# Splitting the input projection's operands engine by engine, and latent queries laid out head by head with their vector step reordered

## The reference, cut to what matters

```
u    = rms_norm(h, ln) @ w_in          # 2048 -> [q latent 512 | kv latent 512 | rotary key 64 | gate 2048]
q    = rms_norm(c_q, ln_q)  @ w_q_up   # 16 heads x (128 plain + 64 rotary)
kv   = rms_norm(c_kv, ln_kv) @ w_kv_up # 16 heads x (128 key + 128 value)
k    = concat([k_plain, k_pe for every head])
q, k = rms_norm(q, g_q), rms_norm(k, g_k)      # over a head's 192 numbers
q, k = rope on the last 64 numbers
h    = h + (causal_attention(q, k, v) * silu(gate)) @ w_o
...                                    # shared keys and values, dilated attention layer
```

## Time and profile before

| what | us |
|---|---|
| median of 3 runs | 1455.38 (1454.78 to 1456.62) |
| the profiled execution, its own time | 1455.89 |
| its span, first to last instruction | 1454.1 |
| PE busy | 1438.4 |
| DVE busy | 856.2 |
| ACT busy | 682.4 |
| POOL busy | 142.7 |

### The profile page before, as it was taken

How to read it: one execution, slowest core, us unless ns; L and a number is a source line. 1 busy time by engine, 2 the same in 40 slices (tenths; PEclk the granted TensorE clock), 3 DMA queues, 4 the chain that set the end, 5 groups by cost and what they waited for, 6 DMA issues and landing times.

```text
span 1454.1 us, 22768 instructions
## 1 busy us (share of the span) xinstructions
PE 1438.4 (99%) x8008; PEld 1253.0 (86%) x8008; DVE 856.2 (59%) x1252; ACT 682.4 (47%) x954; POOL 142.7 (10%) x74
## 2 busy tenths in 40 slices
PE   8999999999999999999999999999999999999998
PEld 5899899999988888888888888888888888888998
DVE  7656766758955555555555555555554565555553
ACT  4555555544444445444444444544544444454432
POOL 5111111100010001000101100100010020010000
PEclk9999999999999999999999999999999999999999
DMA  8554444455565645554554554565455455456454
GB/s 312 168 167 134 135 139 139 138 159 194 181 201 189 193 148 173 196 170 156 189 181 146 188 190 145 172 202 164 156 191 187 145 180 195 146 174 198 150 171 134
DMA packets 70209, 250.61 MB, mean 172 GB/s; under 512 B 7792, under 2 KB 8176, under 8 KB 70000
## 3 DMA queue, kind: packets, MB, share of 16 engines
q1 hardware_dynamic: 69984, 248.38, 52.5%
q10 hardware_dynamic: 144, 1.05, 0.2%
HBM read 247.30 MB, written 2.10 MB: 172 GB/s over the span
## 4 chain that ended last, share of the span: by engine, by line
PE 81%; issue 14%; DVE 2%; POOL 1%; DMA 1%; SPq 0%; ACT 0%; POOLq 0%; ACTq 0%
PE acc L1095 74%; PE turn L1127 2%; PE pv_bank L1139 2%; PE score L1320 2%; POOL rms L395 1%; DVE xa_lo L716 1%; DMA res<-in_xT 0%; DVE xa_hi L713 0%; DMA raw<-in_w_in 0%; DVE w_lo L701 0%; PE og_bank L1147 0%; PE score L1212 0%; PE score L1214 0%; POOL w_lo L385 0%; PE turn L1198 0%
## 5 line engine op out<-in xcount | busy, mean ns | idle before, releaser
L701 DVE TENSOR_TENSOR w_lo<-raw,w_hi 128x1024 fp32r<-128x1024 f32 (+1 forms) x458 | 573.3, 1262 | 421.3 <-ACT w_hi L454 420.6
L454 ACT ACTIVATE w_hi<-raw 128x1024 fp32r<-128x1024 f32 x464 | 484.4, 1050 | 335.7 <-PE acc L1095 318.9
L1095 PE MATMUL acc<-w_hi,xa_hi 128*128 128x512 f32 (+1 forms) x1088 | 407.2, 374 | 8.8 <-POOL w_lo L385 4.2
L1095 PE MATMUL acc<-w_hi,xa_lo 128*128 128x512 f32 (+1 forms) x1088 | 398.0, 366 | 0.0
L1095 PE MATMUL acc<-w_lo,xa_hi 128*128 128x512 f32 (+1 forms) x1088 | 397.1, 365 | 0.0
L1095 PE MATMUL acc<-w_hi,xb_hi 128*128 128x512 f32 (+1 forms) x640 | 250.5, 391 | 1.1 <-issue 1.0
L1095 PE MATMUL acc<-w_hi,xb_lo 128*128 128x512 f32 (+1 forms) x640 | 246.1, 385 | 0.0
L1095 PE MATMUL acc<-w_lo,xb_hi 128*128 128x512 f32 (+1 forms) x640 | 245.6, 384 | 0.0
L1095 PEld LDWEIGHTS acc<-w_hi,xa_hi 128*128 128x128 f32 x1088 | 205.6, 189 | 44.5 <-issue 12.5
L1095 PEld LDWEIGHTS acc<-w_hi,xa_lo 128*128 128x128 f32 x1088 | 205.4, 189 | 33.7
L1095 PEld LDWEIGHTS acc<-w_lo,xa_hi 128*128 128x128 f32 x1088 | 205.8, 189 | 30.9
(11 more groups left out here) (136 smaller groups left out, 973.8 us busy)
## 6 DMA issues: line engine op xcount, KB each, us to landing
raw<-in_w_b SPq DMA_DIRECT2D x320, 512.0 KB, 3.4
raw<-in_w_gate SPq DMA_DIRECT2D x32, 512.0 KB, 3.3
raw<-in_w_out_a SPq DMA_DIRECT2D x32, 512.0 KB, 3.5
raw<-in_w_out_b SPq DMA_DIRECT2D x32, 512.0 KB, 3.6
raw<-in_w_kv SPq DMA_DIRECT2D x16, 512.0 KB, 3.4
raw<-in_w_in SPq DMA_DIRECT2D x15, 512.0 KB, 5.9
raw<-in_w_q SPq DMA_DIRECT2D x16, 384.0 KB, 3.0
out_T<-res SPq DMA_DIRECT2D x8, 256.0 KB, 4.3
```

Of the source, the lines that this page charges most:

```text
L454: nc.scalar.activation(w[0][:, s, 0:width], raw[:, s, 0:width], ACT.Copy).then_inc(hi_ready, 1)
L701: nc.vector.tensor_tensor(w[1][:, s, 0:width], raw[:, s, 0:width], w[0][:, s, 0:width].bitcast(F32), ALU.subtract).then_inc(lo_ready[0], 1)
L1095: last = nc.tensor.matmul(out, x(a), y(b), start=start and k == 0, stop=stop and k == 2, **more)
```

## The change

**Input projection.** The input is loaded in eight pieces of two chunks (`x_two`), into areas that are free at that time (`kT`, `qT`, `v`, `rows`), one ahead of each weight step; the token-major copy goes to `res`, after the weight loads of steps 7 to 10, and `res` is loaded with the transposed input afterwards (four loads of 512 KB behind the load of step 16, `res_loaded`). ACT makes every high half, of the input too (`x_highs`, two ACTIVATE a step with the gain as scale), DVE every low half (`x_lows`, two SCALAR_TENSOR_TENSOR a step); POOL splits nothing. There is one semaphore for low halves. SP issues the first piece of the input ahead of the gains, and ACT issues the two halves of weight step 0. `WARM` becomes 2. PE's step 0 begins with the products of high halves and waits for each low half where it is used. The sums of the kv latent are made at step 11, its rows at 12, its transposes after steps 13 and 14.

**Latent queries.** The query product keeps each head's 192 columns together. The sums are one reduction (two and an addition before), the rows one TENSOR_TENSOR of 128x768 (two before); the rotation reads the rows in place and writes columns 384 to 511. The low half that stood at s = 7 in DVE's list, ahead of the query rows, now stands between the rows and the rotation.

```diff
-WARM = 3
-LOW_0 = 13
+WARM = 2
...
+            load_x(0)
             sp.dma_start(gain[:], gains).then_inc(gains_loaded, 16)
+            load_x(1)
+            for n in range(1, 2 * 8):
+                load(n, n, w_in[n], STEP)
+                if n + 1 < 8:
+                    load_x(n + 1)
...
+                if 7 <= n < 7 + 2 * TILES:
+                    sp.dma_start(tok_parts[n - 7], x_tok[n - 7]).then_inc(tok_loaded[n - 7], 16)
             load(16, 16, w_pe, KC * ROPE)
+            for m in range(2 * TILES):
+                sp.wait_ge(tok_squares, m + 1)
+                sp.dma_start(res[:, 4 * m:4 * m + 4], xT[:, 4 * m:4 * m + 4]).then_inc(res_loaded, 16)
...
-            lows(1, 1)
-            lows(3, 3)
-            for n in range(IN_STEPS):
-                if n == 7:
-                    stream_rms(0)
-                    chain(0, TILES)
-                if n == 15:
-                    chain(1, TILES)
-                if n + 4 < LOW_0 and n % 2:
-                    lows(n + 4, n + 4)
+            stream_rms(0)
+            chain(0, TILES)
+            chain(1, TILES)
...
+            act.dma_start(raw[:, 0, 0:STEP // 2], w_in[0, :, 0:STEP // 2]).then_inc(first_full, 16)
+            act.dma_start(raw[:, 0, STEP // 2:STEP], w_in[0, :, STEP // 2:STEP]).then_inc(raw_full[0], 16)
+
+            def x_highs(m):
+
+                act.wait_ge(x_loaded[m], 16)
+                for c in (2 * m, 2 * m + 1):
+                    last = nc.scalar.activation(xa[0][:, c], x_chunk(c), ACT.Copy, scale=gn("a_ln")[:, c:c + 1])
+                last.then_inc(x_split, 1)
...
+            def x_lows(m):
+
+                dve.wait_ge(x_split, m + 1)
+                for c in (2 * m, 2 * m + 1):
+                    last = nc.vector.scalar_tensor_tensor(
+                        out=xa[1][:, c], in0=x_chunk(c), scalar=gn("a_ln")[:, c:c + 1], in1=xa[0][:, c].bitcast(F32),
+                        op0=ALU.mult, op1=ALU.subtract)
+                last.then_inc(x_ready, 1)
...
+            for n in range(1, 8):
+                x_lows(n)
+                lows(n, n)
...
             def mla_query_sums(i):
...
                 nc.vector.tensor_reduce(ss[:, 0, 0:4].rearrange("p (t u) -> p t u", t=TILES),
-                                        rows[:, (MLA_CHAIN_0 + 1) % 2, :, 0:256].rearrange("p t (u d) -> p t u d", u=2), AX_X, ALU.add)
...
+                                        rows[:, buf, :, 0:2 * QK].rearrange("p t (u d) -> p t u d", u=2),
                                         AX_X, ALU.add).then_inc(sums, 1)
                 dve.wait_ge(sums, c + 1)
-                nc.vector.tensor_tensor(ss[:, 1, 0:4], ss[:, 0, 0:4], ss[:, 0, 4:8], ALU.add).then_inc(pe_sums, 1)
...
-                chain_rows(c, buf, pair, 2, P)
-                nc.vector.tensor_tensor(rot, acc[:, pair, :, 256:384].rearrange("p t (u d) -> p t u d", u=2),
-                                        rms_of(2, ROPE), ALU.mult).then_inc(rot_step, 1)
+                chain_rows(c, buf, pair, 2, QK).then_inc(rot_step, 1)
...
                     if s == 0 and later:
                         mla_query_rows(i - 1, 1 - par)
+                        lows((i, MLA_STEPS), MLA_0 + 3)
                         mla_query_rotate(i - 1)
...
                     if s == 7:
                         mla_query_sums(i)
-                    lows((i, MLA_STEPS), MLA_0 + 4 + s, Q_STEP if s in (2, 3) else STEP)
+                    else:
+                        lows((i, MLA_STEPS), MLA_0 + 4 + s, Q_STEP if s in (2, 3) else STEP)
...
+            pe.wait_ge(x_split, 1)
+            pe.wait_ge(first_hi, 1)
+            for a, b in ((0, 0), (1, 0), (0, 1)):
+                if a:
+                    pe.wait_ge(x_ready, 1)
+                if b:
+                    pe.wait_ge(first_lo, 1)
...
```

More of the change, by code:

```diff
@@ L225, in squares_of, with x_chunk, x_two @@
             return rows[:, j % 2].rearrange("p t (a k) -> p (t a) k", a=2)
-        tok_parts = [rows[:, 0].rearrange("p t k -> p (t k)"), rows[:, 1].rearrange("p t k -> p (t k)"),
-                     kT[:, 0:D // 2], qT[:, 0:D // 2]]
+        x_parts = [kT[:, 0:4 * SEQ], qT[:, 0:4 * SEQ], v[:, 0:4 * SEQ], rows[:, 1].rearrange("p t k -> p (t k)")]
+        tok_parts = [res[:, 4 * m:4 * m + 4].rearrange("p c k -> p (c k)") for m in range(2 * TILES)]
+        def x_chunk(c):
+            return x_parts[c // 4][:, (c % 4) * SEQ:(c % 4 + 1) * SEQ]
+        def x_two(m):
+            return x_parts[m // 2][:, (m % 2) * 2 * SEQ:(m % 2 + 1) * 2 * SEQ].rearrange("p (c k) -> p c k", c=2)
         def reduced(j):
@@ L319, in _, with load_x @@
         def _(sp):
-            sp.dma_start(gain[:], gains).then_inc(gains_loaded, 16)
-            def load_x(j):
-                sp.dma_start(res[:, 4 * j:4 * j + 4], xT[:, 4 * j:4 * j + 4]).then_inc(x_loaded[j], 16)
+            def load_x(m):
+                sp.dma_start(x_two(m), xT[:, 2 * m:2 * m + 2]).then_inc(x_loaded[m], 16)
             def load(n, static_n, src, width):
@@ L328, in load @@
                 if static_n >= RING:
-                    signal, count = low_of(n - RING if isinstance(n, int) else n, static_n - RING)
-                    sp.wait_ge(signal, count)
+                    sp.wait_ge(lo_ready, step_count(n, static_n) - (RING - 1))
                 sp.dma_start(raw[:, s, 0:width], src).then_inc(raw_full[s], 16)
[L333 to L344, removed]
+            load_x(0)
+            sp.dma_start(gain[:], gains).then_inc(gains_loaded, 16)
+            load_x(1)
[3 more added lines that the diff above has]
+                    load_x(n + 1)
+                if n == 7:
                     sp.dma_start(ident[:], identity).then_inc(loaded, 16)
                     sp.dma_start(phase[:, 0:N_MLA_CONSTS], consts).then_inc(loaded, 16)
+                if 7 <= n < 7 + 2 * TILES:
+                    sp.dma_start(tok_parts[n - 7], x_tok[n - 7]).then_inc(tok_loaded[n - 7], 16)
             load(16, 16, w_pe, KC * ROPE)
+            for m in range(2 * TILES):
+                sp.wait_ge(tok_squares, m + 1)
+                sp.dma_start(res[:, 4 * m:4 * m + 4], xT[:, 4 * m:4 * m + 4]).then_inc(res_loaded, 16)
             with sp.Fori(0, PAIRS) as i:
@@ L379, in _ @@
             pool.wait_ge(set_up, SET_UPS)
[L381 to L386, removed]
             def stream_rms(g):
@@ L714, in scaled_stream @@
                 dve.wait_ge(x_hi, k + 1)
-                for c in range(chunks):
+                for c in range(4):
                     last = nc.vector.scalar_tensor_tensor(out=lo[:, c], in0=src[:, c], scalar=g[:, c:c + 1],
@@ L997, in add_stream @@
                 dve.wait_ge(slot_used, step_0 + OUT_FILL_END[j] + 1)
+                if not h_0 and j == 0:
+                    dve.wait_ge(res_loaded, 16 * 2 * TILES)
                 for a in range(2):
@@ L1452 @@
     w_gate = np.stack([slots(gate_cols[:, i * 256:(i + 1) * 256], 4) for i in range(PAIRS)])
-    q_up = a["a_w_q_up"][0].reshape(LORA, PAIRS, 2, QK)
-    w_q = np.stack([slots(np.concatenate([q_up[:, i, :, 0:P].reshape(LORA, 256),
-                                          q_up[:, i, :, P:].reshape(LORA, 128)], axis=1), 2)
-                    for i in range(PAIRS)])
+    q_up = a["a_w_q_up"][0].reshape(LORA, PAIRS, 2 * QK)
+    w_q = np.stack([slots(q_up[:, i], 2) for i in range(PAIRS)])
     def out_slots(w):
```

138 lines of the change are left out of this document (67 added, 71 removed).

## The result

The changed kernel takes 1448.55 us (median of 5, 1447.38 to 1449.59) against 1456.62 for the kernel before in the same comparison: 8.1 us less, ratio 0.995 with a 95% interval of 0.9939 to 0.996. The forecast was 10.0 us less (1445.4, range 1442.8 to 1449.8), reckoned from a median of 1455.38, so 1.2 of the 3.1 us by which the time itself is off belongs to the kernel before and 1.9 to the gain. The sign, the places and the range held; the start of the input projection gave less than its term of the sum. The profiled execution has a span of 1446.6 us where the one before had 1454.1.

The account below looks back on a forecast made before the run. PE was taken to bound the kernel, busy 1438.4 of 1454.1 us. Gains of 7.4 us in the input projection and 2.6 at pair borders sum to 10.0: 1445.4 us against a median of 1455.38, range 1442.8 to 1449.8.

Parts of the forecast that it names:

- the start of the input projection: Input projection up to step 11: step 11 starts at 38.3 instead of 45.67, 7.4 us less.
- Steps 1 to 10 without stalls: Input projection: all engines and loads keep under PE's 2.74 us a step, so 3.6 us of stalls go.
- Step 1's start: Input projection: PE starts step 1 at 10.9 instead of 12.74, with bounds of 10.2 and 11.8.
- The lower clock: PE's 2.2 us idle before step 1: taken not to lower the clock; if it did, at most 1.9 us lost.
- Rival B: Step 1 of the input projection: the lower clock comes again, 1.9 us less gain, 1447.3 us; chance 0.22.
- The border between pairs: Between head pairs: PE's 0.74 us wait goes, 0.25 to 0.4 returns at key transposes; 0.36 a loop pair, 2.6 in all.
- the spare of 0.12 at the key transposes: Key transposes: PE took the key rows 0.15 us after they ended, 0.12 of it to spare without the signal.
- Pair 1: First border between head pairs: its smaller wait goes whole, 0.4 us.
- Rival C: Key transposes take back nearly all of the border's gain: 7.4 + 0.7 us won, 1447.3 us; chance 0.10.
- D: Input projection: loads can't keep the pace, 3.3 us a step for six steps, 3 us back, 1448.4 us; chance 0.12.
- F: Reloads of `res` hold up the first pair's weights; slower than before, 1460 us; chance 0.05.
- E: Input projection: stalls only change owner, as ACT has splits, squares and copies; no change, 1453 to 1458 us; chance 0.06.

Follow-up runs that it names:

- all_lows_dve: Kernel before the change, with only POOL's six low halves of the input projection given to DVE: 1451.37 us, ratio 0.9972.
- table_warm3: Changed kernel with a tiny ACTIVATE ahead of ACT's first wait and three matmuls ahead of step 0: step 1 starts at 10.87, 12.46 without; time not in the text.
- table: Changed kernel with a tiny ACTIVATE ahead of ACT's first wait: step 1 starts at 11.14, 12.46 without; time not in the text.
- warm3: Changed kernel with three instead of two matmuls ahead of step 0: step 1 starts at 11.72, 12.46 without; time not in the text.
- key_low: Changed kernel with the key chain's low half moved behind the key rows: lowest time 1444.29 us, median not in the text; kernel before 1456.12.
- the three kernels of the query part: Kernel before with the whole latent-query part, only its moved low half, or only its layout; times not in the text, the layout alone gave 0.33 us a pair.
- one_queue: Changed kernel with SP again issuing step 0's weights: step 1 came 0.17 us earlier; time not in the text.

## Why the prediction was right, and where it was off

**Steps 1 to 10 without stalls.** Right. No stall, 2.72 a step for 2.74; DVE's splits of the input took 0.87 to 0.88 a pair throughout. That POOL's splits made the stalls was argued from a few rows; all_lows_dve showed it, with 4.5 us, and showed DVE's splits at their short price again.

**Step 1's start.** This is the term of the sum that was mis-sized: 10.9 forecast, 12.46 measured. The two assumptions under it failed. The first piece of the input landed 4.3 us after its issue and not 3.3, as ACT's transfers now ran beside it, and ACT's table load of 1.28 us, which ran at the start before, stood behind it. Neither was on the path in the forecast, whose path to step 1 was load (8.6), high half, low half. In the changed kernel ACT made the high half at 9.05 without an idle before it, behind its splits of the input, and the low half was ready at 11.44: 0.5 later than forecast. The other 1.0 is PE itself, which the sum left out: it took step 0 to end near 8.6, and step 0 ended at about 12.4, late by its start at 7.97 and slow by the clock. With both edits of table_warm3 step 1 starts at 10.87, the forecast's 10.9.

**The lower clock.** The forecast took "not" and was wrong, though the place was not the one it looked at. It expected an idle of 2.2 us after step 0; there was none, but one of 2.31 ahead of it, from the late input and one warm matmul less. table and warm3 each take it away and bring step 1 to 11.14 and 11.72. Rival B's condition thus came true, a lower clock before step 1, but its gain of 8.1 us, which is just the measured one, is in part luck: it priced the clock at 1.9, where warm3, which removes little else, gained 0.7 at step 1. The table load, the late piece and the smaller gain in the pairs made up the rest.

**The border between pairs.** The mechanism was right in each link: power 1.01, `ms` and DVE's later work 0.25 earlier, the wait of 0.74 gone at the border and one of 0.2 to 0.4 back at the key transposes. The gain of a loop pair was 0.24 and not 0.36. The term that was wrong is the spare of 0.12 at the key transposes: it was read from the matmul's start, 0.15 behind the key rows, but the weight load ahead of that matmul needs the rows first, and it started only 0.05 to 0.06 behind them in each of pairs 2 to 7, as close as in the changed kernel, where it is held by them. With no spare, a pair can win only what the key rows win, which was 0.25. Pair 1 gave 0.2 where 0.4 was forecast (key power 6.30 earlier than before at pair 1, 6.10 at pair 0's). All pairs together gave 7.9 - 6.1 = 1.8 instead of 2.6. Rival C, the key transposes taking back nearly all, left only 0.7 for the pairs, where 1.8 came; its total of 8.1 fits only because the input gave 1.4 less.

**What the forecast did not separate.** It put the gain on the two edits together. The layout alone makes it; the moved low half is worth nothing until the key chain's low half is moved too.

**The other rivals.** The loads kept the pace (D): 356 to 415 GB/s in the windows from 5 to 16 us. The reloads of the residual hid (F) and ACT kept up (E): behind step 0, PE's list of waits has no wait for a weight step.

## What to carry to other kernels

When a wait on a chain of engines goes, time the next consumer of the same chain before counting the gain; here it gave back two thirds (0.24 us a pair won of the 0.68 that key_low shows). Keep a long VectorE instruction like the low half (1.23 us) from starting just ahead of a short GpSimd step on the critical chain, and try it for all such steps of the loop together, as one of two gave nothing here. Measure a small spare at the first instruction that needs the data: here the weight load, not the matmul. At a kernel's start, look at what stands behind the first wait of each engine: a table load, the gains, the idle that lowers the clock.

## What the runs showed of the hardware

- The power on POOL (128x4) takes 1.01 us when it starts ahead of a DVE low half and 1.91 to 1.99 when it starts just behind one (0.16 us in the rows above). Between the kernels above, moving the low half changed the one into the other in every loop pair. A low half that starts behind the power does not lengthen it: in all_lows_dve one power started at 122.76, the low half at 122.91, and the power took 1.01.
- The slow pace of matmuls (0.43 us apart) came after idles of 2.92 and 2.31 us in the input projection (and of 2.61, 2.99 and 3.61 in the three kernels of the query part), and not after 1.86, 1.78, 1.30 and 1.14. The length of the idle alone does not decide it: in one_queue step 0 ran at that pace after an idle of 1.05. There the granted clock reads 1.00, so the pace has to be looked at beside it.
- A table load need not be at the start of ScalarE's program. In the kernel before it ran at 0.74 us; with another first ACTIVATE it began at 5.10 or, in one_queue, at 3.86, each time when the first input piece had landed. Why the place differs was not settled. An ACTIVATE that waits for nothing long, put first, brought it to 1.68.
- Gains of 96 KB issued second landed late enough (5.96 in `table`) to hold back ScalarE's first split, behind 512 KB issued before them.
